# One unit less split ahead of its expert block: AHEAD from 5 to 4, in a two-block transformer kernel

## What is computed

```python
for e in range(N_EXPERTS):
    a = jax.nn.silu(h @ lp['w_gate'][e]) * (h @ lp['w_up'][e])
    y = y + combine[..., e, None] * (a @ lp['w_down'][e])
```

## Time and profile before

| | us |
|---|---|
| median of three runs | 2004.54 (2000.44 to 2005.87) |
| the profiled execution: its time | 2005.87 |
| its span, first to last instruction | 2004.4 |
| PE busy | 1822.2 (91%) |
| DVE busy | 1215.0 (61%) |
| ACT busy | 890.9 (44%) |

### The profile page before, as it was taken

One profiled execution on the slowest core, in us unless ns is written; L12 is line 12 of the kernel. 1 busy time (PEld: TensorE's weight loads), 2 busy tenths in 40 slices (PEclk: granted clock), 3 DMA queues, 4 the chain that ended last, 5 costly groups with the idle time before them and its releaser, 6 DMA issues. The chain is left out here.

```text
span 2004.4 us, 25531 instructions
## 1 busy us (share of the span) xinstructions
PE 1822.2 (91%) x9172; PEld 1514.9 (76%) x9172; DVE 1215.0 (61%) x2158; ACT 890.9 (44%) x1430; POOL 107.5 (5%) x127
## 2 busy tenths in 40 slices
PE   7997899999998986889999999799968879999993
PEld 6776788888887764778888888686667868888882
DVE  3554668887224547358866422655572468988985
ACT  2446443322223436343222312433562358888883
POOL 1000000000000000001100000200000011011001
PEclk7998999999998998989999999699989579999997
DMA  4223224545332214125654333320212169999993
GB/s 145 85 74 112 84 62 138 146 138 146 106 95 74 63 53 168 44 62 158 182 154 137 105 95 95 101 78 1 75 47 81 63 239 378 387 374 370 364 362 144
DMA packets 203999, 289.85 MB, mean 145 GB/s; under 512 B 12348, under 2 KB 150564, under 8 KB 203780
## 3 DMA queue, kind: packets, MB, share of 16 engines
q1 hardware_dynamic: 188932, 240.08, 36.1%
q0 software_dynamic: 11920, 36.48, 5.9%
q10 hardware_dynamic: 3056, 12.06, 1.6%
HBM read 271.77 MB, written 22.05 MB: 147 GB/s over the span
## 5 line engine op out<-in xcount | busy, mean ns | idle before, releaser
L227 DVE TENSOR_TENSOR weights_low<-ring,weights_high 128x1024 fp32r<-128x1024 f32 x202 | 246.7, 1223 | 410.1 <-ACT weights_high L221 409.9
L200 PE MATMUL bank<-XH,weights_high 128*128 128x512 f32 x1120 | 455.9, 407 | 34.5 <-DVE XL L69 20.3
L202 PE MATMUL bank<-XH,weights_low 128*128 128x512 f32 x1120 | 446.0, 398 | 0.0
L201 PE MATMUL bank<-XL,weights_high 128*128 128x512 f32 x1120 | 445.1, 397 | 0.0
L221 ACT CAST weights_high<-ring 128x1024 fp32r<-128x1024 f32 x202 | 211.4, 1048 | 442.2 <-PE bank L202 441.8
L200 PEld LDWEIGHTS bank<-XH,weights_high 128*128 128x128 f32 x1120 | 216.3, 193 | 83.1 <-ACT squares L69 12.3
L202 PEld LDWEIGHTS bank<-XH,weights_low 128*128 128x128 f32 x1120 | 215.4, 192 | 47.2
L201 PEld LDWEIGHTS bank<-XL,weights_high 128*128 128x128 f32 x1120 | 216.3, 193 | 43.4 <-issue 0.5
L2130 DVE TENSOR_TENSOR XL<-ring,XH 128x1024 fp32r<-128x1024 f32 x144 | 169.7, 1221 | 12.5 <-ACT XH L2124 12.5
L2124 ACT CAST XH<-ring 128x1024 fp32r<-128x1024 f32 x144 | 145.1, 1048 | 0.3 <-PE bank L202 0.3
L69 DVE SCALAR_TENSOR_TENSOR squares<-ring,c_silu,squares 128x128 f32<-128x128 f32 x384 | 135.2, 352 | 13.6
(11 more groups left out here) (472 smaller groups left out, 3112.7 us busy)
## 6 DMA issues: line engine op xcount, KB each, us to landing
ring<-in_w_ffn_in SPq DMA_DIRECT2D x88, 512.0 KB, 4.8
ring<-in_w_gate SPq DMA_DIRECT2D x72, 512.0 KB, 5.6
ring<-in_w_up SPq DMA_DIRECT2D x72, 512.0 KB, 7.4
ring<-in_w_down SPq DMA_DIRECT2D x72, 512.0 KB, 6.4
ring<-in_w_ada POOLq DMA_DIRECT2D x48, 512.0 KB, 4.7
ring<-in_w_ffn_out SPq DMA_DIRECT2D x44, 512.0 KB, 3.5
ring<-in_w_out SPq DMA_DIRECT2D x24, 512.0 KB, 3.6
slot_output<-expert_out SPq DMA_DIRECT2D x19, 512.0 KB, 6.8
```

Of the source, the lines that this page charges most:

```text
L200: PE.matmul(out_ap, w_h, x_h, start=first, stop=False, skip_group_check=True)
L201: PE.matmul(out_ap, w_h, x_l, start=False, stop=False, skip_group_check=True)
L202: return PE.matmul(out_ap, w_l, x_h, start=False, stop=last, skip_group_check=True)
L227: V.tensor_tensor(wl[:, s, :], ring[s][:, :], wh[:, s, :].bitcast(F32), ALU.subtract).then_inc(split_done.sem, 1)
```

## The change

`AHEAD` goes from 5 to 4: units 0 to 3 instead of 0 to 4 are split ahead of a block, and the calls in `block` follow, with every unit still split once. Unit 4 is now split inside its own block, behind the output copies of the block before. The table load with its probe, until now the first thing on ACT in a block, goes behind the four splits at the gate products and that of unit 8. In the back part the unit index moves by one, so the next block's rows are again split behind unit 11 and behind unit 0 of the next block.

```diff
-HELD, AHEAD = 6, 5
+HELD, AHEAD = 6, 4
...
             reach(PE, l_silu, b)
-            reach(S, l_table, b)
-            S.activation(table_in[:, :], ones[0:1, 0:1], ACT.Silu).then_inc(l_table.sem, 1)
             for q in range(4):
                 split_ahead(q)
                 gate(q)
+            split_ahead(4)
+            reach(S, l_table, b)
+            S.activation(table_in[:, :], ones[0:1, 0:1], ACT.Silu).then_inc(l_table.sem, 1)
             reach(S, l_used, b * UNITS + 4)
             reach(S, l_av, b * 2)
             S.activation(sg[:, :], bank[0][:, :], ACT.Silu).then_inc(l_silu.sem, 1)
             reach(PE, l_av, b * 2)
-            split_ahead(4)
+            split_ahead(5)
             unit_high(b, 10)
...
-            for q in range(6, UNITS):
+            for q in range(7, UNITS):
                 split_ahead(q)
-                if q in (6, 7) and not last:
-                    split_rows(b + 1, q - 6)
+                if q < 9 and not last:
+                    split_rows(b + 1, q - 7)
```

## The result

The changed kernel took 2012.30 us (median of 7 runs, 2010.37 to 2017.41), the kernel before 2004.42 (median of 7, 1998.92 to 2005.87). The ratio of the means is 1.0051, with a 95% interval of 1.0037 to 1.0065: slower by 0.5%, about 10 us (7 to 13; the two medians are 7.9 us apart). I had given 2004.5 and a range up to 2009.5.

The account below looks back on a forecast made before the run. PE was taken to bound the expert blocks at 18.8 us each; all terms were 0, so 2005.87 us for the profiled execution stayed, given as a 2004.5 us median, range 1998.5 to 2009.5.

Parts of the forecast that it names:

- The total is the same list.: ScalarE's work in a steady block: same items, only three change places, so the block stays 18.8 us, term 0.
- The slower rival: Idle time ahead of the moved table load makes Silu, unit 9's split and the hidden product late; 4 in 100.
- delay g: Idle time ahead of the moved load: first 0.7 us free, rest counted 18 times, decisive from 1.03 us.
- 0.89 us: Idle time ahead of the last block's table load, taken as a possible delay: 3.4 us slower, 2007.9 us.
- Output copies: ScalarE at the block's turn: sign that these copies come about 0.95 us earlier against the block's first matmul.
- Silu within 0.2 us of before: ScalarE mid-block: sign that Silu, behind the moved load, starts at 1826.43 where it was 1826.42.
- The 0.51 us of VectorE ahead of unit 5 gone: VectorE in each block: sign that its idle 0.51 us ahead of unit 5's low half disappears.
- Unit 4 late: Unit 4 split inside its block: low half still ready 1.4 us before PE wants it, no cost.
- ends of the loop: First and last block: hidden product's inputs ready 1.2 and 0.4 us in hand, term 0 for both.
- transfers at nothing: Fetches of up units: term 0, bounds -1.4 and 0, the 1.4 us from one copy less beside the first gather.
- The faster rival: VectorE sets PE's pace through an unnamed wait, so 0.51 us per block is won: 8.7 us, 1995.8; 5 in 100.
- A rule on the load: Table load costs 1.30 us with no extra drain; the skill's added 1380 ns drain would give about 2017 us.

Follow-up runs that it names:

- e1: Changed kernel with the Silu probe moved back to the head of the block, AHEAD still 4, one table load; ratio 1.0002 to the kernel before.
- e6: As e1, with one added ScalarE copy of 1024 columns between high 8 and Silu, output unused; ratio 1.0022 to the kernel before.
- e7: As e1, with two added ScalarE copies of 1024 columns between high 8 and Silu, outputs unused; ratio 1.0094 to the kernel before.
- e8: Changed kernel with both table loads, unit 9 split ahead of the second load; ratio 0.9991 to the kernel before.
- e2: Kernel before, AHEAD still 5, only the Silu probe moved behind the four gate splits, two table loads; ratio 1.0065 to the kernel before.

## Why the prediction was wrong

- **The step that failed** is the one that reads "The total is the same list." ScalarE's list has one item more. I asked whether the load would stay at its probe or go to the head of the iteration, worked out both, and never their sum. It is both: the code is a loop body, its first ScalarE operation is now a cast, and a load was put ahead of that cast; the probe behind then brought a second one, 1.28 us long, and Silu and high 9' came 1.42 us later in ScalarE's loop, where the sum had them in place. Before, the probe stood first and its load served both. That casts need no load of their own behind Silu's is seen in the earlier trace rows and in e1.
- **The price** was nearly right, under the wrong heading. The slower rival said: of a delay g the first 0.7 us are free, the rest counts 18 times, and it decides from 1.03 us on. Measured: 0.76 us free, the slope is 1 (e6, e7), and g is 1.42 us. There are 18 blocks, not 19, so the rest counts 17 times at most: (1.42 - 0.76) x 17 = 11.2 us, against 10.7 us in the traces (the 12.3 us less the 1.6 of the clock), and 7 to 13 us by the interval. Only I looked for g in idle time ahead of a load, not in a second load, and gave it 4 in 100; the range's upper end came from 0.89 us and missed.
- **The chain of that rival** (Silu, high 9', low 9', hidden product late) is the one that happened, shown by e8, which takes high 9' out of it.
- **Output copies** 0.95 us earlier against the block's first matmul: right. They start 1.25 us after it before (1820.13 less 1818.88) and 0.31 us after it now (1820.31 less 1820.00).
- **Silu within 0.2 us of before**: wrong, by the second load. It starts 8.98 us after the first matmul (1828.98 less 1820.00), where it was 7.54 (1826.42 less 1818.88).
- **The 0.51 us of VectorE ahead of unit 5 gone**: right as such; in its place stand 0.62 us ahead of unit 4 and 0.95 us ahead of unit 9, both behind a load.
- **Unit 4 late, ends of the loop, transfers at nothing**: e1 has them all with the probe at the head, and its ratio is 1.0002 (0.9992 to 1.0013). Of the gather's possible 1.4 us nothing was seen: from POOL's first copy of the token numbers (tokens_now) to the first gate matmul it is 14.2 us before, 14.7 in e1 and 14.3 after. PE's step from block to block is 0.44 us (1819.56 to 1820.00), where it was 0.46.
- **The faster rival**: nothing for it. VectorE's idle 0.51 us went and PE's period did not fall (e1, e8).
- **A rule on the load.** The second load starts 0.02 us after high 8' has ended (1826.50 plus 1.05) and its probe 1.30 us later: there is no separate drain in the new place either. The Trainium skill, "ScalarE: Activation LUTs", section "What ACT_TABLE_LOAD costs", has the 1283 ns right and adds 1380 ns that no run here shows; the time that it gave, 2017, came nearer to the result than mine, but for another reason, a whole second load. The Trainium skill's page "ScalarE activation tables: per-element evaluation and per-set limits", section "Table sets in the compiler and the runtime", says that loads are placed per block by the greedy longest run. If a loop's body is such a block, the first part agrees: each iteration has its load. A run that counted the casts along with Silu would have made one load of two, and the traces of after and e2 have two.

What stays open: which table set the load at the head brings, and by what rule it is put there. The traces name no set, and no run had another first operation than a cast, Silu or Exp.

## What to carry to other kernels

Where a list of instructions is only put in another order, ask what is generated between them. In every run here the first ScalarE operation of the loop body had a table load ahead of it; with the Silu probe there, that one served the whole block, and with a cast there, the probe brought a load of its own. An engine with idle time may still have almost no slack, if its idle time lies inside a loop of waits: add up the loop (here 18.05 us against PE's 18.81), not the busy share (16.04 of 18.8). And when a rival's price per microsecond is known, price every source of delay with it, an added instruction first of all.

## What was not expected of the hardware

The load behaves as 1.28 us of plain ScalarE time in all three places where a steady block had one (behind the output copy at the loop's turn, behind a cast, behind another probe), with at most 0.03 us to its neighbours, apart from the 0.1 us or so of overlap between two casts that it takes away (1.07 us from the start of a cast to the load, 0.95 us to another cast). At the last block, behind the loop, 0.89 us of idle time stood ahead of it before and 1.90 after, a pause that no steady block has.
